# Second block's residual and the last branch product's first half held in the place of attention's keys

## What is computed

```
merged = gates[:, :, 0] * y_a + gates[:, :, 1] * y_b
x = x + merged @ w_out[l]

xn2 = rmsnorm(x, norm_ffn_g[l])
gu = xn2 @ w_ffn_in[l]
ff_gate, ff_up = jnp.split(gu, [D_FF_2], axis=-1)
x = x + (jax.nn.silu(ff_gate) * ff_up) @ w_ffn_out[l]
```

## Time and profile before

| what | value |
|---|---|
| three runs | 3432.08, 3435.79, 3438.52 us; median 3435.79 us |
| profiled execution | 3434.82 us, its span 3433.5 us, mean granted clock 0.979 |
| PE busy | 3268.7 us (95%) |
| DVE busy | 1930.0 us (56%) |
| ACT busy | 1375.0 us (40%) |
| POOL busy | 384.0 us (11%) |

### The profile page before, as it was taken

The page is one execution under the profiler, slowest core; times in us unless marked ns, Lnnn a source line. Parts: engine busy times, 40 slices in busy tenths (PEclk is TensorE's granted clock), DMA queues, the critical chain, the costliest instruction groups (busy, mean ns, idle before and its releaser), DMA issues. The chain is left out here.

```text
span 3433.5 us, 39601 instructions
## 1 busy us (share of the span) xinstructions
PE 3268.7 (95%) x14862; PEld 2660.0 (77%) x14862; DVE 1930.0 (56%) x3098; ACT 1375.0 (40%) x2320; POOL 384.0 (11%) x605
## 2 busy tenths in 40 slices
PE   6999999989999999999999999998788899999998
PEld 3888888877788878888888888877556678888886
DVE  4474343454334387777445455655676587777443
ACT  4592232224333243333233355554566343333221
POOL 0121000001100200000011101111211200001011
PEclk8999999999999999999999999999999899999999
DMA  5365443344553323323762434445744523335752
GB/s 218 110 215 184 141 126 123 123 159 158 201 162 111 129 88 115 117 105 132 251 206 80 153 118 144 138 150 152 168 97 99 186 89 117 106 116 166 248 179 75
DMA packets 228045, 494.14 MB, mean 144 GB/s; under 512 B 21520, under 2 KB 84624, under 8 KB 226320
## 3 DMA queue, kind: packets, MB, share of 16 engines
q1 hardware_dynamic: 147728, 302.30, 27.7%
q0 software_dynamic: 80128, 189.30, 16.9%
HBM read 353.63 MB, written 137.89 MB: 143 GB/s over the span
## 5 line engine op out<-in xcount | busy, mean ns | idle before, releaser
L290 PE MATMUL p<-s_xh,s_wh 128*128 128x512 f32 x2256 | 903.2, 400 | 34.6 <-DVE s_tmp L401 12.3
L291 PE MATMUL p<-s_xl,s_wh 128*128 128x512 f32 x2256 | 886.2, 393 | 0.0
L292 PE MATMUL p<-s_xh,s_wl 128*128 128x512 f32 x2256 | 885.7, 393 | 0.0
L290 PEld LDWEIGHTS p<-s_xh,s_wh 128*128 128x128 f32 x2256 | 428.9, 190 | 128.6 <-issue 21.7
L292 PEld LDWEIGHTS p<-s_xh,s_wl 128*128 128x128 f32 x2256 | 428.2, 190 | 91.7
L291 PEld LDWEIGHTS p<-s_xl,s_wh 128*128 128x128 f32 x2256 | 429.1, 190 | 88.9 <-issue 1.7
L2089 PE MATMUL p<-s_xh,s_wh 128*128 128x512 f32 x1152 | 451.5, 392 | 15.0 <-DVE s_wl L2330 15.0
L2091 PE MATMUL p<-s_xh,s_wl 128*128 128x512 f32 x1152 | 450.1, 391 | 0.0
L2090 PE MATMUL p<-s_xl,s_wh 128*128 128x512 f32 x1152 | 450.1, 391 | 0.0
L250 DVE TENSOR_TENSOR s_wl<-s_ws,s_wh 128x1024 fp32r<-128x1024 f32 x157 | 195.4, 1257 | 237.9 <-ACT s_wh L242 237.5
L2089 PEld LDWEIGHTS p<-s_xh,s_wh 128*128 128x128 f32 x1152 | 217.6, 189 | 61.1 <-issue 16.3
(11 more groups left out here) (380 smaller groups left out, 5102.8 us busy)
## 6 DMA issues: line engine op xcount, KB each, us to landing
d_h<-s_fhl POOLq DMA_DIRECT2D x80, 512.0 KB, 3.4
s_ws<-i_Wf SPq DMA_DIRECT2D x48, 512.0 KB, 4.3
s_qb<-i_Wf SPq DMA_DIRECT2D x40, 512.0 KB, 4.0
s_qb<-i_Wf SPq DMA_DIRECT2D x80, 256.0 KB, 3.0
s_ws<-i_Wf SPq DMA_DIRECT2D x80, 256.0 KB, 2.8
s_aw<-i_adaT SPq DMA_DIRECT2D x32, 512.0 KB, 3.7
s_xh<-d_h POOLq DMA_DIRECT2D x16, 1024.0 KB, 12.4
s_xl<-d_h POOLq DMA_DIRECT2D x16, 1024.0 KB, 14.9
```

The costliest lines, as they stand in the source:

```text
L290: pe.matmul(o, wh, H[:, k, c:c + n], start=(k == 0), stop=False)
L291: pe.matmul(o, wh, L[:, k, c:c + n], start=False, stop=False)
L292: last = pe.matmul(o, wl, H[:, k, c:c + n], start=False, stop=(k == 7))
```

## The change

Two new buffers, `X2` and `PART` (8 x 512 floats a partition each, 16 KB a partition each), are placed where the keys lie. What the change does:

- the products m = 4 to 7 of `wo2` are a new kind "kept": ACT copies them from PSUM into `PART` (after the last scores, `sc_mm.at(128)`), and neither the store to `dW2` nor the read back takes place;
- the stored products m = 0 to 3 are read into `PART` instead of `RES`, and the residual's first half for all 8 tiles into `X2`; these 12 reads wait for the last scores, not for the end of stage 6, and stand in SP's list ahead of the load of P2's weight tiles;
- the residual's second half is read into `X2` as well, tile m as soon as the first half's tile m is summed, all 8 ahead of the load of P3's weight tiles; `lq` is not used in this stage;
- DVE adds `X2` and `PART` into `RES`; ACT and DVE make P2's weight tiles between the fourth and the fifth tile, P3's ahead of the root of the sums;
- on PE the sums of the first half move from P1, k = 6, to P2, k = 2, and the spread from P2, k = 4, to k = 6; the second-half sums of P2 move within the norm from its tile 3 to its tile 6.

The core of the diff:

```diff
@@ fill_act
+        if p.kind == "kept":
+            out, free = p.dst
+            ACW.wait_ge(*free)
+            ac.activation(out, ps, ACT.Copy).then_inc(*evA.up())
+            return
@@ stage6
+        X2, PART = placed(([128, 8, 512], F, "x2half"), ([128, 8, 512], F, "parthalf"))
...
-        items += [("wo2", m, "new first", "plain", dW2, "wo2", 1.0, TC) for m in range(8)]
+        items += [("wo2", m, "new first", "plain", dW2, "wo2", 1.0, TC) for m in range(4)]
+        items += [("wo2", m, "new first", "kept", (PART[:, m, :], sc_mm.at(128)), "wo2", 1.0, TC) for m in range(4, 8)]
@@ stage7
-        n0 = plan_norm(0, [ready[(i, 0)] for i in range(8)], attended.y0, {3: lambda: plan_after(pairs[2])})
+        n0 = plan_norm(0, [ready[(i, 0)] for i in range(8)], attended.y0, {6: lambda: plan_after(pairs[2])})
...
         def sp_():
-            weights_sp(ahead(pairs[0][0].i, 2) + NS)
-            for t in gone:
-                SPW.wait_ge(*t)
-            for f in first:
-                residual_sp(f.q, f.free, f.m, 0)
-                for t in written[("wo2", f.m)]:
-                    SPW.wait_ge(*t)
-                sp.dma_start(RES[:, f.m, 0:512], dW2[f.m][:, 0:512]).then_inc(*part_in[f.m % 4].up())
+            SPW.wait_ge(*attended.scores)
+            for m in range(8):
+                residual_sp(m, 0)
+                if m < 4:
+                    for t in written[("wo2", m)]:
+                        SPW.wait_ge(*t)
+                    sp.dma_start(PART[:, m, :], dW2[m][:, 0:512]).then_inc(*part_in[m].up())
+            weights_sp(ahead(pairs[0][0].i, 2) + NS)
+            for m in range(8):
+                SPW.wait_ge(*summed.at(m + 1))
+                residual_sp(m, 1)
             for js in pairs:
                 weights_sp(ahead(js[0].i, 2) + NS)
-                for j in js:
-                    residual_sp(j.q, j.lq_free, j.m, 1)
 
         def pe_():
             products_pe(pairs[0])
-            products_pe(pairs[1], {6: lambda: sums_pe(s0)})
-            products_pe(pairs[2], {4: lambda: spread_pe(0, DIA[:, 0, :], s0.diag, n0.q[7])})
+            products_pe(pairs[1])
+            products_pe(pairs[2], {2: lambda: sums_pe(s0), 6: lambda: spread_pe(0, DIA[:, 0, :], s0.diag, n0.q[7])})
             products_pe(pairs[3])
...
+        def first_dve(f):
+            DVW.wait_ge(*parts[f.m])
+            DVW.wait_ge(*x2_in[f.m].at(1))
+            dv.tensor_tensor(RES[:, f.m, 0:512], X2[:, f.m, :], PART[:, f.m, :], ALU.add).then_inc(*summed.up())
+            if f.m:
+                square_dve(squares[(f.m - 1, 0)], squares[(max(f.m - 2, 0), 0)].sum, ACC)
...
             weights_dve(ahead(pairs[0][0].i, 2))
-            for f in first:
...
+            for f in first[:4]:
+                first_dve(f)
+            weights_dve(ahead(pairs[1][0].i, 2))
+            for f in first[4:]:
+                first_dve(f)
             square_dve(squares[(7, 0)], squares[(6, 0)].sum, ACC)
             after_dve(pairs[0])
+            weights_dve(ahead(pairs[2][0].i, 2))
             sums_dve(s0, DIA[:, 0, :], [])
-            weights_dve(ahead(pairs[1][0].i, 2))
             after_dve(pairs[1])
-            weights_dve(ahead(pairs[2][0].i, 2))
-            norm_dve(n0, lambda i: vec("nf2", i), None, {3: lambda: after_dve(pairs[2])})
+            norm_dve(n0, lambda i: vec("nf2", i), None, {6: lambda: after_dve(pairs[2])})
             weights_dve(ahead(pairs[3][0].i, 2))
             after_dve(pairs[3])
```

More of the change, by code:

```diff
@@ L344, in plan_fill @@
                     store_planned(p.slot2, (key, m))
+                elif kind == "kept":
+                    pass
                 elif kind == "turned":
@@ L3257, in stage6 @@
         done.gone, done.scores, done.y0 = ended(), sc_mm.at(128), jobs[-1].mm
+        done.x2, done.part, done.parts = X2, PART, [p.ev for p in jobs[12:]]
         retire(*key_in, *q_in, *zb_in, *mb_in, v_in, ad_in, padded, negated, sc_mm, biased, sink_d, exps, divided, turned, copied, weighed, gated, merged,
@@ L3275, in stage7 @@
             pairs.append(js)
-        part_in = [sig("in", f"part{s}") for s in range(4)]
+        X2, PART = attended.x2, attended.part
+        part_in, x2_in = [sig("in", f"part{m}") for m in range(4)], [sig("in", f"x2_{m}") for m in range(8)]
         summed = sig("dv", "first_half")
         ready, squares = {}, {}
[L3279 to L3287, removed]
+        parts = [s.at(1) for s in part_in] + attended.parts
         first = []
@@ L3291, in stage7 @@
             f = Plan()
-            f.m, f.part, f.done = m, part_in[m % 4].due(), summed.due()
-            f.q, f.free, f.arrived = plan_gate(f.done)
+            f.m, f.done = m, summed.due()
             ready[(m, 0)] = f.done
@@ L3299, in plan_after @@
             for j in js:
-                j.q, j.lq_free, j.arrived = plan_gate(j.ev)
                 ready[(j.m, 1)] = j.ev
@@ L3344, in act_ @@
             weights_act(ahead(pairs[0][0].i, 2))
-            for f in first:
+            for f in first[:4]:
+                square_act(squares[(f.m, 0)], ACC, [])
+            weights_act(ahead(pairs[1][0].i, 2))
+            for f in first[4:]:
                 square_act(squares[(f.m, 0)], ACC, [])
             after_act(pairs[0])
+            weights_act(ahead(pairs[2][0].i, 2))
             sums_act(s0)
-            weights_act(ahead(pairs[1][0].i, 2))
             after_act(pairs[1])
-            weights_act(ahead(pairs[2][0].i, 2))
-            norm_act(n0, None, {3: lambda: after_act(pairs[2])})
+            norm_act(n0, None, {6: lambda: after_act(pairs[2])})
             weights_act(ahead(pairs[3][0].i, 2))
@@ L3358, in after_dve @@
                 DVW.wait_ge(*j.mm)
-                DVW.wait_ge(*j.arrived)
-                dv.tensor_tensor(RES[:, j.m, 512:1024], B[j.bank][:, :], lq[:, j.q, :], ALU.add).then_inc(*evD.up())
+                DVW.wait_ge(*x2_in[j.m].at(2))
+                dv.tensor_tensor(RES[:, j.m, 512:1024], B[j.bank][:, :], X2[:, j.m, :], ALU.add).then_inc(*evD.up())
+        def first_dve(f):
[4 more added lines that the diff above has]
+                square_dve(squares[(f.m - 1, 0)], squares[(max(f.m - 2, 0), 0)].sum, ACC)
         def dve_():
@@ L3365, in dve_ @@
             weights_dve(ahead(pairs[0][0].i, 2))
-            for f in first:
-                DVW.wait_ge(*f.part)
-                DVW.wait_ge(*f.arrived)
-                y = RES[:, f.m, 0:512]
-                dv.tensor_tensor(y, y, lq[:, f.q, :], ALU.add).then_inc(*summed.up())
-                if f.m:
-                    square_dve(squares[(f.m - 1, 0)], squares[(max(f.m - 2, 0), 0)].sum, ACC)
+            for f in first[:4]:
+                first_dve(f)
+            weights_dve(ahead(pairs[1][0].i, 2))
+            for f in first[4:]:
+                first_dve(f)
             square_dve(squares[(7, 0)], squares[(6, 0)].sum, ACC)
             after_dve(pairs[0])
+            weights_dve(ahead(pairs[2][0].i, 2))
             sums_dve(s0, DIA[:, 0, :], [])
-            weights_dve(ahead(pairs[1][0].i, 2))
             after_dve(pairs[1])
-            weights_dve(ahead(pairs[2][0].i, 2))
-            norm_dve(n0, lambda i: vec("nf2", i), None, {3: lambda: after_dve(pairs[2])})
+            norm_dve(n0, lambda i: vec("nf2", i), None, {6: lambda: after_dve(pairs[2])})
             weights_dve(ahead(pairs[3][0].i, 2))
@@ L3397, in stage7 @@
         pool_()
-        retire(*part_in, summed)
+        retire(*part_in, *x2_in, summed)
         return half_done(ready, s1, pairs[3][1].mm, lambda i: vec("nf2", i), None)
```

5 lines of the change are left out of this document (2 added, 3 removed).

## The result

The changed kernel takes **3423.58 us** in the median of 6 runs (3420.19 to 3428.58), beside 3436.6 us of the kernel before (6 runs, 3431.6 to 3438.6). The ratio is 0.9965, 95% interval 0.9952 to 0.9978: 7.6 to 16.5 us less. So it is faster, as forecast, but 10.6 us above the forecast of 3413 and outside the range of 3408 to 3420. The profiled execution of the changed kernel took 3420.19 us.

The account below looks back on a forecast made before the run. PE bounds the kernel, busy 3268.7 of 3433.5 us. Of 23.5 us lost in stage 7, less 0.5 remaining wait, 23.0 come off 3434.82, leaving 3411.8; stated as 3413 on the median's scale, range 3408 to 3420.

Parts of the forecast that it names:

- account of what there was to win: Stage 7, from P1's end to the second half's sums: 23.5 us lost to PE's waits and lower clock.
- Step 1: The 12 reads start at about 2667.2 instead of 2676.6 us; DVE's 7.74 us wait goes to zero.
- Step 2: P2's weight tiles between fourth and fifth sum: last squares in at about 2690.7, 3.7 us ahead of the sums' place.
- rival C: Transfers bound the first half: PE waits 1.2 us at the sums, 2.1 more at the spread; 3419 us; chance 0.12.
- Step 3: P3's loads land 3.9 us after issue at 2690.4; diagonal ready at 2699.2, 1.6 us ahead of the spread.
- B: Root late: P3's tiles take 6.8 instead of 3.9 us, PE waits 1.3 at the spread; 3415.5 us; chance 0.18.
- Step 4: Norm and feed-forward tiles: PE waits about 0.4 us around the first plain group, 0.5 with the refill.
- Step 5: Second-half sums no longer wait for `lq` and come before the group after needs anything; no cost was counted.

Follow-up runs that it names:

- e2: Changed kernel with P3's weight loads issued between the fourth and fifth second-half reads; 3417.03 us, ratio 0.9947 to the kernel before.
- e5: Changed kernel with P2's loads ahead of first-half reads 4 to 7 and P3's ahead of second-half reads 4 to 7; 3416.69 us.
- e9: Changed kernel with P3's loads ahead of second-half reads 4 to 7 and POOL's first-half stores behind the second half's; 3419.45 us.
- e7: Changed kernel with SP issuing P2's loads first, then waiting for the end of stage 6 before the 12 reads; 3426.55 us.
- e3: Changed kernel with P2's weight loads issued between the fourth and fifth first-half reads; 3420.06 us, ratio 0.9955 to the kernel before.
- e4: Changed kernel with POOL's eight stores of the first half's sums issued behind those of the second half; 3417.0 us.
- e8: Changed kernel with all eight second-half residual reads behind P3's weight loads in SP's list; 3419.61 us.
- second profile: Changed kernel profiled once more without an edit; 3420.84 us, stretch from P1's low parts to the second half's sums 59.00 us.
- e6: Changed kernel with all eight first-half products stored to DRAM and read back, none kept; 3426.49 us.
- e1: Changed kernel with the root, reciprocal and diagonal made ahead of P3's weight tiles on ACT and DVE; 3424.93 us.

## Why the prediction missed

**The account of what there was to win held.** PE's places came out to the hundredth: the sums 21.17 us behind P1's low parts (forecast 2694.42 less 2673.25) and 21.17 measured; the spread 27.57 against 27.56 in e2, e5 and e9. With both loads moved the stretch is 54.26 against 53.4; PE's own work in it is 53.5 for 52.9.

**Step 1, Earlier reads: right, but worth less than it looks.** The reads go out at 2668.92, 5.4 us ahead of P1's low parts (forecast 6.0), and the first sum waits for none of them; the third waits 0.37. e7 says what this start and the later place of P2's loads are worth together: 2 to 4 us, the lower end hardly more than scatter. Where P2's tiles are not late, the start is worth 6 (e7 against e3).

**Step 2, P2's weights in the middle: right in its result, wrong in a term.** PE doesn't wait ahead of the sums. But the second tile is in 12.7 us behind P1's low parts, not 8.95. The windows of the changed kernel (last column GB/s):

```profile
2668.00:2676.00 8.00, 8.00 (x37) 6.62 (x36) 2.43 (x4) 3.13 (x4) 0.00 (x0) 1.00 0.81 244
2676.00:2682.00 6.00, 6.00 (x28) 4.99 (x27) 4.44 (x7) 2.50 (x4) 2.21 (x4) 1.00 1.04 397
2682.00:2688.00 6.00, 6.00 (x29) 4.95 (x28) 1.22 (x1) 2.06 (x2) 0.00 (x0) 1.00 1.01 399
```

Until 2687.0 that is 1.95 + 2.38 + 2.00 = 6.3 MB, from 2668.9 on at 350 GB/s in the mean, for the 368 that I took. So the rate was nearly right and the bytes were not: I had given P2's tiles what stands ahead of them and two stores, 5.2 MB. Four stores and four reads of the second half were issued while the tiles were under way. That these bytes made the tile late is shown only in part. Of the 3.8 us, the stores' part is 1.1 by e4 against the first profile, 0.4 against the second, 1.7 by e9 against e2. In e8, without the reads, the tile was in no sooner, at 2687.52, and in the two us before that hardly a byte moved (39 GB/s):

```profile
2685.60:2687.50 1.90, 1.90 (x11) 1.55 (x10) 0.70 (x1) 1.06 (x1) 0.00 (x0) 1.00 0.10 39
```

So in e8 the shared rate doesn't explain the last stretch of the wait; what held the tile's last packets no run shows, and most of the 3.8 us stays unassigned. The squares had 3.7 us to spare and used nearly all: the last ended at 2694.93, 0.5 ahead of the sums, so that rival C's wait of 1.2 there stayed out narrowly.

**Step 3, Root and P3's weights: the step that failed.** The forecast has the diagonal 25.95 us behind P1's low parts; it was there at 32.27. Of these 6.3 us, 2.5 are the issue of P3's loads (19.65 for 17.15), passed on from step 2 by the eighth sum. The other 3.9 are their landing, and here a term of the sum was mis-sized: 7.8 us instead of 3.9 (7.1 in the second profile). The 3.9 came from the earlier trace rows, from two loads in the kernel before, ahead of which no byte moved from 2674.0 to 2675.4 and beside which POOL issued no store (its next came at 2684.61); here six stores of POOL were issued around these two. With two stores instead of six (e4) the first load was in after 4.6 us, so the stores are 3.2 of the 3.9, or 2.5 by the second profile. What is left of the 3.9 isn't assigned; four reads stood right ahead of these loads. From there it follows: less the spare 1.6, PE waits 4.6 at the spread. And then 2.0 at the lower clock, of which the forecast had nothing and rival C "at most the 2.46 of before". It came with the long waits: behind the spread's waits of 2.88 (e7) and 3.36 (e6) the matmuls start at the slow pace, too, behind those of 1.35 (e3) and 1.66 (e8) at the full one. PE's own 53.5, the spread late by 4.7, 2.0 for the clock and 0.4 ahead of the plain group make 60.6 of the 60.73. Three experiments take lateness away by three means, the loads' place (e2), the loads ahead of them (e3, in part) and the stores (e4), and gain 4.4 to 5.5 against the first profile, 2.7 to 3.8 against the second.

The rivals had the mechanism. B put P3's tiles 2.9 later with 1.3 us of wait at the spread; C put step 2 late and had 1.2 at the sums and 2.1 at the spread. What happened is B's late landing on top of C's late issue, which I priced as alternatives. Neither needs the other: in e3 the loads were issued 15.9 us behind P1's low parts, sooner than forecast, and the first still took 7.8 us. B's own remark "with a slower step 2 it is 3" came nearest, but did not go into its time. By the rule of the Trainium skill that rival C names ("DMA: Bandwidth & Descriptors", section "Queues, rings and completion order"), queues are served in turn, packet by packet. The trace agrees in direction: with six stores of another queue beside them two 512 KB loads took 8.1 us, with two 4.9. I had applied the rule to P2's tiles alone, where it mattered least.

**Step 4, Norm and feed-forward tiles: nearly right.** Forecast 0.5 of wait; 0.78 in e5 and 0.76 in e9, where nothing ahead is late. That it has no cover showed in e1: P3's low parts held up the norm, and PE waited 5.18.

**Step 5, Second-half sums: right.** They cause no wait in any run of the changed kernel but e8.

**The rest of the miss lies ahead of stage 7.** 3423.58 is 10.6 above the forecast; the stretch accounts for 7.3 in one profile and for 5.6 in the other. The kernels' medians less their stretch, less 683.9 and 1.3, put P1's low parts at 2675.6 before (3436.6, with the mean of both stretches, 75.8) and at 2678.5 after (3423.58 and 59.9). Profiles of the changed kernel and its variants range from 2671.30 to 2682.07, of the kernel before there are two. Whether these 3 us are an effect of the change on earlier stages or chance stays open; one source of the scatter is shown in the last section. They are a part of what separates the gain in the stretch, 16, from that in the medians, 13.

The lowest median is that of e5: 3416.69 us, 15.8 to 24.4 less than before; e2 (3417.03) and e4 (3417.0) can't be told from it. The changed kernel with two calls moved in SP's list wins another 4.7 to 6.5 us of stretch; in run time their intervals (0.9929 to 0.9954, 0.9952 to 0.9978) barely overlap, and none of its five runs (3414.8 to 3419.51) reaches the lowest of the changed kernel's, 3420.19.

## What to carry to other kernels

A load in a queue is not done when what stands ahead of it is done: count what runs beside it too, above all where the row that its price is read from had no such company. Here another queue's stores made up 2.5 to 3.2 us of one landing; that a load's own successors delay it was not shown (e8). When a list is pushed forward, put the loads that a critical engine needs next ahead of the reads that wait for that engine, not behind the last of them. And two lateness rivals that share a chain are not alternatives: price them together.

## What the runs showed of the hardware

**The same wait sometimes costs the clock and sometimes not.** In stage 6 PE waits 1.51 to 1.54 us for a tile of DVE at the same point in every profile. In both profiles of the kernel before, in e2, e7 and e9 the four transposes behind it take 0.68 us and PE goes on at full clock. In the other eight profiles they take 0.87 to 1.09, and the matmuls behind run at the lower level: in the changed kernel 6 start in 2.71 us from 2639.67 (granted clock 0.50), where before 6 take 1.47 from 2640.02 (granted clock 1.00). In the 3.1 us ahead of the transposes PE was busy for as long in both, 1.35 and 1.34 us; why the one falls and the other doesn't is not shown. That is one visible source of the scatter ahead of stage 7.

```profile
2639.09 0.93 PE L3098 MATMUL p<-s_ident,s_pr 128*128 128x128 f32 x4 [1.51 <-DVE s_pr L3195]
```

**A subtraction of DVE takes longer while POOL adds.** In e2 the norm's first subtraction (L1573) takes 1.83 us instead of 0.69, while an addition of POOL runs from 2702.99 to 2704.29; in e5, where this addition has ended ahead of the norm, the same one takes 0.69. The difference, 1.14, is that of their waits ahead of the first plain group (1.71 and 0.58). In e3, e4 and e8 the addition meets the norm's second subtraction, which takes 1.13 to 1.14 instead of 0.69, and the waits are 1.03 to 1.05, again the same difference. The product between the two (L1564), which reads PSUM, takes 0.74 in e4 beside the same addition of POOL, as without it. DVE's and POOL's timelines in e2:

```profile
2703.02 1.83 DVE L1573 TENSOR_TENSOR s_xl<-s_tmp,s_xh 128x512 fp32r<-128x512 f32 x1
```

```profile
2702.99 1.30 POOL L1466 TENSOR_TENSOR s_acc<-s_acc,s_tmp 128x512 f32<-128x512 f32 x1
```

That DVE, in an operation with two inputs in SBUF, and GpSimd hold a common port in turn, the whole instruction long, is what the Trainium skill states in "SBUF — State Buffer", section "SBUF: two separate sides". The trace agrees: in e2 the subtraction ends 0.56 us after POOL's addition, about its own 0.69.
